# First layer of a two-layer MoE backbone: the order of the experts' steps is changed

## The reference

```python
for e in range(N_EXPERTS):
    y = (jax.nn.silu(t @ w_gate[e]) * (t @ w_up[e])) @ w_down[e]
    out = out + combine[:, e:e + 1] * y
```

## Time and profile before

| | |
|---|---|
| median of 3 runs | 1363.06 us (1361.83 to 1367.06) |
| the profiled execution, its time | 1368.47 us |
| its span in the trace | 1366.7 us |
| mean granted TensorE clock | 0.961 |
| TensorE busy | 1248.4 us (91%) |
| first layer's expert steps | from 486.7 us to about 805 us of the span |

### The profile page before, as it was taken

The page is one execution under the profiler, slowest core; times in us unless marked ns, Lnnn a source line. Parts: engine busy times, 40 slices in busy tenths (PEclk is TensorE's granted clock), DMA queues, the critical chain, the costliest instruction groups (busy, mean ns, idle before and its releaser), DMA issues.

```text
span 1366.7 us, 20148 instructions
## 1 busy us (share of the span) xinstructions
PE 1248.4 (91%) x8220; PEld 790.9 (58%) x8220; DVE 624.7 (46%) x1130; ACT 369.3 (27%) x599; POOL 124.9 (9%) x119
## 2 busy tenths in 40 slices
PE   4799999999999898999999966999999989998986
PEld 1477678787777633433333336787789845443443
DVE  2728467786455542121131116476876671221222
ACT  2523224352254300010100015444455520000000
POOL 0000000000023020000000020006940310000000
PEclk9799999999999899999999987999999999999998
DMA  9734469463535569899899983785254679999997
GB/s 378 282 142 190 180 233 382 146 225 124 231 139 219 215 263 374 304 344 348 327 349 399 415 339 132 295 352 216 93 157 169 255 307 392 385 390 392 393 420 294
DMA packets 59760, 382.34 MB, mean 280 GB/s; under 512 B 8880, under 2 KB 11380, under 8 KB 20180
## 3 DMA queue, kind: packets, MB, share of 16 engines
q1 hardware_dynamic: 45584, 345.00, 65.2%
q10 hardware_dynamic: 9652, 18.47, 4.2%
q0 software_dynamic: 4432, 17.58, 3.5%
HBM read 363.45 MB, written 44.84 MB: 299 GB/s over the span
## 4 chain that ended last, share of the span: by engine, by line
PE 23%; issue 22%; DMA 11%; DVE 5%; ACT 2%; POOL 2%; SPq 0%; DVEq 0%; ACTq 0%; POOLq 0%
DMA wexp<-in_expert 8%; PE bank L2467 4%; PE bank L2046 3%; PE bank L2047 3%; PE bank L2048 3%; PE bank L2482 3%; DMA x_rows<-trow,rowid 2%; PE bank L2014 2%; PE bank L2500 1%; PE bank L2056 1%; POOL m_lo L764 1%; DMA stage<-in_in 1%; PE bank L2326 1%; PE bank L2138 1%; DVE xT L1275 1%
## 5 line engine op out<-in xcount | busy, mean ns | idle before, releaser
L2467 PE MATMUL bank<-wexp,xg 128*64 128x512 f32 (+1 forms) x1488 | 266.4, 602 | 10.7 <-DMA wexp<-in_expert 7.7
L2046 PE MATMUL bank<-h_hi,whi 128*128 128x512 f32 (+1 forms) x640 | 226.5, 354 | 14.4 <-DVE h_lo L1269 11.9
L2048 PE MATMUL bank<-h_hi,wlo 128*128 128x512 f32 (+1 forms) x640 | 220.9, 345 | 0.0
L2047 PE MATMUL bank<-h_lo,whi 128*128 128x512 f32 (+1 forms) x640 | 220.9, 345 | 0.0
L2467 PEld LDWEIGHTS bank<-wexp,xg 128*64 128x64 f32 (+1 forms) x1488 | 77.9, 126 | 163.5 <-issue 145.7
L2482 PE MATMUL bank<-wexp,act_a 128*32 128x256 f32 (+1 forms) x1072 | 145.6, 488 | 18.8 <-DMA wexp<-in_expert 12.0
L1269 DVE TENSOR_TENSOR wlo<-stage,whi 128x2048 fp32r<-128x2048 f32 x56 | 133.2, 2386 | 37.9 <-ACT whi L807 36.3
L2046 PEld LDWEIGHTS bank<-h_hi,whi 128*128 128x128 f32 x640 | 125.1, 195 | 38.5 <-issue 14.2
L2047 PEld LDWEIGHTS bank<-h_lo,whi 128*128 128x128 f32 x640 | 125.3, 196 | 13.7 <-issue 0.5
L2048 PEld LDWEIGHTS bank<-h_hi,wlo 128*128 128x128 f32 x640 | 124.8, 195 | 14.0
L1269 DVE TENSOR_TENSOR act_a<-act_s,bank 128x256 f32<-128x256 f32 (+1 forms) x47 | 17.1, 365 | 243.9 <-ACT act_s L807 243.9
(11 more groups left out here) (345 smaller groups left out, 1632.7 us busy)
## 6 DMA issues: line engine op xcount, KB each, us to landing
wexp<-in_expert SPq DMA_DIRECT2D x190, 1024.0 KB, 14.5
stage<-in_in SPq DMA_DIRECT2D x40, 1024.0 KB, 8.5
raw<-in_mod SPq DMA_DIRECT2D x18, 1024.0 KB, 6.8
stage<-in_mod SPq DMA_DIRECT2D x16, 1024.0 KB, 4.8
x_rows<-in_c_zero SPq DMA_DIRECT2D x32, 512.0 KB, 7.6
y_rows<-in_c_zero SPq DMA_DIRECT2D x20, 512.0 KB, 7.8
spare<-in_mod SPq DMA_DIRECT2D x8, 1024.0 KB, 17.0
stage<-in_out SPq DMA_DIRECT2D x8, 1024.0 KB, 4.8
```

The source lines that it names most:

```text
L2046: MM(o, w[0], x_[0], start=start, stop=False)
L2047: MM(o, w[0], x_[1], start=False, stop=False)
L2048: return MM(o, w[1], x_[0], start=False, stop=stop)
L2467: ins = MM(bank[0][g * w:(g + 1) * w, :], x_[:, 2 * j + k, :], weights[:, c], start=(first_ == 0), stop=(last_ == 0))
```

## The change

The order of the first layer's steps is another permutation of the same 27, and the place in SP's order at which three modulation units are issued moves from before chunk (5, 0) to before chunk (6, 0).

```diff
-ORDER = ((0, 1, 3, 3, 9, 3, 10, 3, 2, 2, 11, 2, 12, 2, 4, 4, 13, 4, 14, 4, 5, 5, 6, 6, 8, 7, 7),
+ORDER = ((0, 1, 5, 5, 3, 3, 3, 3, 9, 10, 2, 2, 2, 2, 11, 12, 4, 4, 4, 4, 13, 14, 6, 6, 8, 7, 7),
          (0, 1, 9, 6, 4, 4, 14, 5, 11, 3, 3, 13, 8, 2, 2, 12, 7, 10))
...
                 for r, j in plan.issue(plan.loads[LEADERS[l]:], 4, EC):
-                    if l < DEPTH - 1 and (r, j) == (5, 0):
+                    if l < DEPTH - 1 and (r, j) == (6, 0):
 
                         sp.wait_ge(S("gu_sb"), 4)
                         for i in range(3):
```

## The result

The changed kernel took 1405.6 us in the median of four runs (1402.0 to 1411.6), the kernel before 1364.4 in the same comparison: ratio 1.0306, 95% interval 1.0258 to 1.0354. The forecast was 1385 with a range of 1370 to 1394: the direction was right, the size was half of what came. Some 8 of the 41 us are in no trace; they are spread between executions. Read by stage the traces fit better. From the start of step 0 to the extra item the stage grew by 38.6 us, and the rest of the program was 5.1 us shorter in the trace after.

What follows compares the result with a forecast made beforehand. TensorE was taken to bound the first layer's expert stage, with DMA close below. Added waits of 31.9 us less 10.2 us of old stalls gave net +21.7 us, from 1363.1 to 1385 us, range 1370 to 1394.

Steps and rivals of the forecast that it cites:

- What bounds: First layer's expert stage: bound by TensorE, with DMA load so close below that it becomes the bound for a while.
- Steps 19 to 23: Down product in step 23 waits for expert 6's fourth chunk, twentieth in SP's queue; 19 us, bounds 11 to 22.
- The single wait of 15 to 20 us in step 23: Expected profile sign: near 770 us the down product waits once for wexp, with a half clock behind it.
- no wait in step 20: Expected profile sign: the old 4.1 us wait of the gate product for expert 5's chunks is gone.
- Steps 7 to 11, and 13 to 17: Sixteen chunks until step 11's down product, hidden by a hair; 1 us, and 1 for the same pattern from step 13.
- Step 4's wait: Expert 9's four chunks delay the y_rows write, so act_a comes late: 5.9 us wait plus 1.7 for the clock.
- Rival (b): Step 4: the y_rows write is not delayed and the wait disappears; +14 us, 1377; chance 0.17.
- Start of step 4: Fetch of step 4's rows, 256 instead of 128 KB, lands later and TensorE waits; 0.8 us, from nothing to 3.
- The sum: Whole kernel: 31.9 us added, 10.2 us of old stalls removed, net +21.7 us; median 1363.1 to 1385.
- (c): Chunk spacing 3.25 us everywhere: stalls of 5.6 twice and 24 in step 23; +32 us, 1395; chance 0.07.
- (d): Chunk spacing 2.61 us everywhere, no wait in step 4: +4 us, 1367, no measurable difference; chance 0.07.
- (e): Queue keeps up at 2.1 us per chunk, no wait in step 23, 10.2 us gained: 1353; chance 0.04.

Runs made afterwards that it cites:

- the run with runs of four alone: Against the kernel before: four steps of experts 3, 2 and 4 in a row, two narrow experts behind each, expert 5 at its old place; 1386.4 us, ratio 1.0149.
- both relocations: Changed kernel with filter tables issued behind the y_rows write and three modulation units before chunk (10, 0); 1390.8 us, ratio 1.0168 to the kernel before.
- The run with the units early: Changed kernel with its three modulation units issued before chunk (10, 0) instead of (6, 0); 1397.4 us, ratio 1.0235 to the kernel before.
- The two parts alone: Kernel before with only expert 5's steps moved to the front, 1381.9 us; or only four steps of experts 3, 2 and 4 in a row, 1386.4 us.

## Why the prediction was wrong

**What bounds, and the tail: right.** Steps 19 to 23 were the largest term. It was reckoned that the chunk for the down product in step 23 comes 61.4 us after the start of step 19; it came after 62.1 (788.10 - 726.02), with the slow clock behind it (5.80 for 3.65, 2.2 us for the 2 taken), and no wait in step 20. The single wait of 15 to 20 us in step 23 did not come as such: it is 12.7 us there and 5.9 in step 22, 18.6 for the 19 forecast. Part of this accuracy is luck. The 60.5 us for twenty chunks was picked between 57.2 and 63.1; by the mean of 2.86 alone the chunk would have been put 4 us too early here too. That bytes make it is shown from both sides: three units fewer in SP's queue, by moving them or by halving expert 14's chunks, bring the chunk 7 us earlier.

**Where it failed: "Steps 7 to 11, and 13 to 17".** The prediction called these transfers hidden by a hair and took 1 us for each. They cost 4.9 + 2.4 and 3.1 + 1.7 us, 12.1 in all: 10 of the missing us. The failing step is the spacing of 2.86 us per chunk, which was a mean over a stretch that is mostly tail, multiplied by the number of chunks. The waits were for the fifteenth chunk, not the sixteenth for which the prediction reckoned; by its own spacing that one was to come 1.7 us ahead of TensorE. In the stretch from 588 to 640 us of the changed kernel the queues have (packets, MB, share of the 16 engines)

```profile
q1 hardware_dynamic: 2396, 17.53, 87.5%
q10 hardware_dynamic: 1156, 2.01, 12.2%
```

17.53 MB are 16.7 chunks, so 3.11 us each, the start from an empty queue included; ScalarE's queue took 12.2% of the engines here and 8.6% from 686 to 804 us before. Fifteen chunks are 46.7 us; the chunk awaited came 49.0 us after the first was issued at 588.4. The other 2.3 us are later chunks, already under way: when the fifteenth had landed, the queue had moved 16.48 MB, 15.7 chunks. So 3.27 us per awaited chunk, and the upper bound of 3.25 that the prediction had in hand was the right value here. It had been read from a stretch that begins, as this one does, with an empty queue, and was set aside for the mean of a long full one. How much of the longer spacing is the wide steps' traffic and how much the start was not told apart by a run. And slow clock came behind both waits: at neither place had it been counted.

**"Step 4's wait": right in mechanism, too small.** The wait was 8.5 for 5.9 us and the slow product 2.4 for 1.7: 3.3 us more. The landing of the write was put at 549 out of 549 to 553, and the trace has 552.8; but step 3 starts 1.65 us earlier in this trace. Counted from the start of step 3 it was put at 23.4 us, at most 27.4, and came after 28.9: its issue was 1.8 us later than before, and it took 23.2 us to land instead of 13.0. That is 10.2 us more, nearly all of the 10.4 us reckoned for the four chunks; the 3.7 us that the prediction took off did not come off. Holding the four chunks back takes 9 us off the landing, moving the tables behind the write takes the wait away, and in the run with runs of four alone, which issues no chunk there, the write had landed within 12.8 us: each of the two is needed for the wait. Rival (b) is out.

**"Start of step 4": the size was off, and the reason covers little of it.** 3.5 us instead of 0.8. The prediction ascribed a possible loss to the block of 256 instead of 128 KB. The block counts for about 1 us: from issue to use it took 6.1 to 7.8 us with 128 KB and, but for the two runs named above, 7.4 to 8.7 with 256. POOL can fetch only when the scatter has landed, and it is this that moves against TensorE. In the kernel before the fetch was issued 0.1 us after the start of step 3, in the changed one 1.9 us after it:

```profile
525.80 1.62 POOL L730 DMA_DIRECT2D xpick<-x_rows  x3 [26.80 <-DMA x_rows<-trow,rowid]
```

In the old order with 128 KB and units before (14, 0) it was 2.7 us after, and the wait 3.4. In the changed order with both relocations, 256 KB, it was issued at 525.26, level with the start of step 3, and the wait is 0.3 us:

```profile
525.25 7.09 PE L2467 MATMUL bank<-wexp,xg 128*64 128x512 f32 x32
532.69 0.71 PE L2014 MATMUL bank<-tables,xpick 64*128 64x64 f32 x8 [0.34 <-DMA xpick<-x_rows]
```

So in eight of the twelve traces, two of the four of the old order among them, the wait is 3.3 us or more, and the trace of before was a favourable draw for it. This would explain why the tables' relocation gave less in the old order than the trace of before promised: the stall of step 4 that it removes was, in other executions, one of step 3, which it does not. In the changed order, though, this wait is no loss of its own. The run with the units early, which up to step 5 is the same program, has 3.8 and 6.5 us for the 3.5 and 8.5, and its write lands 28.9 us after the start of step 3 too; both took 77.0 us to step 5. The late write bounds both steps, and what TensorE doesn't wait for in step 3 it waits for in step 4. Why the scatter ends at another time from one execution to the next is open.

**The sum.** The stage grew by 38.6 us for the 21.7 forecast: 10.1 more from the middle, 6.0 from steps 3 and 4, 0.7 from the tail. The two parts alone (15 and 20 us) make 35 of the 41 us of both, and by the length of the stage 17.0 and 18.6 of the 38.6. That is near a sum and fits losses at separate places, but the rest is within the spread of the medians and was not told apart. Of the medians' 41 us, the part above the traces' 33.5 stays open too; the changed kernel's four executions spread over 9.6 us.

**Rivals.** (c), the slow spacing everywhere, was nearest with 1395. Its own terms, 0.8 + 7.6 + 5.6 + 5.6 + 24 + 2 + 0.5 - 10.2, make 36 us and not 32, so 1399; the upper end of the range was drawn 4 us too low by this, and the result lies beyond either. Its 3.25 us held in the middle but not in the tail, where the awaited chunk was the twentieth in 61 us, 3.06 each. (d) and (e) asked for 2.61 and 2.1 us per chunk; from 732 to 788 us, with the engines full, SP's queue moved 20.74 MB, 2.84 us per chunk.

## What to carry to other kernels

In this kernel, two slots and a queue in order mean that a long user of one slot lets one successor be loaded and then idles the engines. Short users behind it must then be loaded in their own short time. Spread them between the long steps, and put bulk loads that are needed late where the queue stands still, after checking what is due next: in the old order the units alone gave 0.35%, and with the tables moved as well it was 0.3 and 0.5%, so that the tables' own share was not told apart. When a deadline is met "by a hair" with a mean rate, use the rate of the nearest stretch with the same neighbours and the same start, add what later transfers have moved when the awaited one lands, and allow for a slow clock behind a wait. Look whether a wait that is near zero in the one trace at hand is near zero in others, and whether another wait would only take its place.

## What the runs showed of the hardware

A DMA issue on SP, 0.33 us as a rule, took 2.3 to 2.6 us when many transfers were under way (from 726 to 789 us the median weight chunk landed 24.8 us after its issue), here in step 21 of the changed kernel, about the time in which a chunk is moved:

```profile
739.46 0.34 SPq L658 DMA_DIRECT2D wexp<-in_expert  x1
...
753.90 2.30 SPq L658 DMA_DIRECT2D wexp<-in_expert  x1
```

It cost nothing here, as the order of the queue stayed the same. Where the clock fell, the loss behind a wait had nearly the same size whatever the wait's length: 1.7 us behind 3.1, 2.4 behind 4.9 and 2.2 behind 12.7 us, in each case one down product that began at the 1.2 GHz level or fell to it and ended back at 2.4. But it did not fall behind every wait: the windows behind 3.45 us in step 3 of the changed kernel, and behind 3.47 and 3.25 us in the run with runs of four alone, have a granted clock of 1.00 throughout, and the products their usual length, while 3.32 us in the old order with the units alone were followed by 0.50 and a product of 5.35 us.
